# Turning the attention's value product, with two heads per step, in a two-block hybrid layer on one Trainium2 core

## The reference, cut to what matters

```python
# 8 heads "a" (window 128, with sinks) and 8 heads "b" with three branches;
# heads of 64, and 4 heads share a key/value group (2 groups of each)
o_a = banded_gqa(qa, ka, v_a, 128, rel_bias[:, :8], sinks)
p_c = softmax(q_b . k_cmp); o_cmp = p_c . v_cmp        # 31 compressed keys
o_sel = softmax(q_b . k_sel + bias) . v_sel            # causal, all 512 keys
o_win = softmax(q_b . k_win + bias) . v_win            # causal, window 512
gb = sigmoid(g_b + b_nsa_gate)                         # a gate per head and branch
o_b = gb0 * o_cmp + gb1 * o_sel + gb2 * o_win
y = concat([o_a * silu(z_a), o_b * silu(z_b)])
out = x + gate * (y @ w_out)
```

## Time and profile before

| | us |
|---|---|
| three executions | 1449.93, 1450.42, 1449.90 |
| median | 1449.93 |
| the profiled execution | 1452.35 |
| its span (first to last instruction) | 1450.6 |
| of it, the attention up to the first tile of `w_out` (195.4 to 315.5) | 120.1 |

### The profile page before, as it was taken

How to read it: one execution, slowest core, us unless ns; L and a number is a source line. 1 busy time by engine, 2 the same in 40 slices (tenths; PEclk the granted TensorE clock), 3 DMA queues, 4 the chain that set the end, 5 groups by cost and what they waited for, 6 DMA issues and landing times.

```text
span 1450.6 us, 18082 instructions
## 1 busy us (share of the span) xinstructions
PE 1424.3 (98%) x6880; PEld 1187.8 (82%) x6880; DVE 742.1 (51%) x1200; ACT 603.1 (42%) x1014; POOL 113.1 (8%) x133
## 2 busy tenths in 40 slices
PE   6999999999999999999999999999999999999998
PEld 5787879998888888888888888888888888888887
DVE  6733678855666434556445344443457433333342
ACT  5624677745333332333333344432355333333221
POOL 5303232100000000000000111100000000000000
PEclk9999999999999999999999999999999999999999
DMA  9996200113433333212213233343332333333321
GB/s 283 318 228 216 65 1 2 59 59 104 159 101 93 109 89 101 87 59 76 77 52 87 71 89 88 101 150 98 87 102 83 106 102 101 88 98 96 105 80 58
DMA packets 227824, 149.69 MB, mean 103 GB/s; under 512 B 5330, under 2 KB 216014, under 8 KB 227108
## 3 DMA queue, kind: packets, MB, share of 16 engines
q1 hardware_dynamic: 223588, 131.63, 31.4%
q0 software_dynamic: 4160, 17.04, 4.1%
HBM read 140.92 MB, written 6.68 MB: 102 GB/s over the span
## 4 chain that ended last, share of the span: by engine, by line
PE 93%; DMA 2%; DVE 1%; SPq 1%; ACT 1%; issue 1%; DVEq 0%; ACTq 0%
PE ps L436 70%; PE ps L2266 6%; PE ps L2292 3%; PE ps L2191 3%; PE ps L1857 3%; DMA w_raw<-in_w_in_dram 2%; PE ps L2278 2%; PE ps L1965 1%; PE ps L1926 1%; PE ps L2177 1%; PE ps L2176 1%; SPq L550 1%; PE ps L1998 0%; SPq L580 0%; PE ps L2146 0%
## 5 line engine op out<-in xcount | busy, mean ns | idle before, releaser
L456 DVE TENSOR_TENSOR w_lo<-w_raw,w_hi 128x1024 fp32r<-128x1024 f32 (+1 forms) x214 | 258.3, 1210 | 255.8 <-ACT w_hi L451 253.1
L451 ACT ACTIVATE w_hi<-w_raw 128x1024 fp32r<-128x1024 f32 (+1 forms) x214 | 219.5, 1034 | 14.7 <-PE ps L436 11.2
L502 ACT ACTIVATE temps<-ps 128x512 f32<-128x512 f32 x67 | 40.0, 597 | 238.8 <-PE ps L436 238.8
L436 PE MATMUL ps<-g_hi,w_hi 128*128 128x512 f32 x384 | 95.8, 392 | 0.0
L436 PE MATMUL ps<-g_hi,w_lo 128*128 128x512 f32 x384 | 94.9, 389 | 0.0
L436 PE MATMUL ps<-g_lo,w_hi 128*128 128x512 f32 x384 | 94.8, 389 | 0.0
L436 PEld LDWEIGHTS ps<-g_hi,w_lo 128*128 128x128 f32 x384 | 72.1, 188 | 15.0
L436 PEld LDWEIGHTS ps<-g_lo,w_hi 128*128 128x128 f32 x384 | 72.1, 188 | 15.0
L436 PEld LDWEIGHTS ps<-g_hi,w_hi 128*128 128x128 f32 x384 | 71.5, 188 | 14.6
L436 PE MATMUL ps<-f_hi,w_lo 128*128 128x512 f32 x288 | 71.1, 389 | 0.0
L436 PE MATMUL ps<-f_hi,w_hi 128*128 128x512 f32 x288 | 71.1, 389 | 0.0
(11 more groups left out here) (448 smaller groups left out, 2738.7 us busy)
## 6 DMA issues: line engine op xcount, KB each, us to landing
w_raw<-in_w_in_dram SPq DMA_DIRECT2D x107, 512.0 KB, 3.9
w_raw<-in_w_ff_gate_dram SPq DMA_DIRECT2D x22, 512.0 KB, 3.7
w_raw<-in_w_ff_up_dram SPq DMA_DIRECT2D x22, 512.0 KB, 3.8
w_ada_shift_scale<-in_w_ada_dram SPq DMA_DIRECT2D x16, 512.0 KB, 8.3
w_raw<-in_w_r_out_dram SPq DMA_DIRECT2D x16, 512.0 KB, 4.5
w_raw<-in_w_ff_down_dram SPq DMA_DIRECT2D x16, 512.0 KB, 3.9
w_ada_gate<-in_w_ada_dram SPq DMA_DIRECT2D x4, 1024.0 KB, 11.6
x_spill<-x_t POOLq DMA_DIRECT2D x2, 2048.0 KB, 10.1
```

The lines of the kernel that those rows point to most:

```text
L436: mm = pe.matmul(bank, w[:, slot, k], mov[:, at_k], start=first and n == 0 and k == 0, stop=last and n == 2 and k == kts - 1)
L451: act.activation(whi[:, slot, 0:kts], raw[:, slot, 0:kts], ACT.Copy).then_inc(hi_done, 1)
L456: nc.vector.tensor_tensor(wlo[:, slot, 0:kts], raw[:, slot, 0:kts], whi[:, slot, 0:kts].bitcast(F32), ALU.subtract).then_inc(lo_done, 1)
L502: act.activation(dst, ps[:, o % 4], func, scale=scale).then_inc(evac, 1)
```

## The change

Heads go two at a time through all engines ("pairs"; 48 of them, and a pair has the same keys and the same value group). The value product is turned: 64 columns of the values are the stationary operand, and the transposed probabilities (128 queries) are the moving one; one head of a pair writes PSUM partitions 0 to 63 and the other 64 to 127, so that the result has the queries on the free axis, as `w_out` needs it. It comes three pairs behind the scores where keys are 128 or 256 wide, two pairs behind where they are wider. The transposes of the finished blocks fall away. The coefficients (one per query and head) must now lie on the free axis: GpSimd widens them to 64 columns (`widen`), TensorE transposes them (4 per group), ScalarE copies them out, and VectorE multiplies with them (`combined`). The gating by silu moves to GpSimd (`y_gate`), save for the last half, which VectorE and GpSimd share. For widths up to 256 the two heads' transposed probabilities share a bank and are copied by one instruction. The compressed probabilities are scaled by GpSimd before their transposes, which move to pair 5; the compressed products come at pairs 8, 9, 11 and 12, two later than elsewhere in this form, and the gates' reciprocal at pairs 2 and 3. SyncE holds the fourth tile of `w_out` until the last value product.

```diff
+CTR_AT = 5
+CO_PE_AT = (8, 9, 11, 12)
+K_WINDOW_AT = (1, 2, 3, 4)
+Y_AT = (16, 19, 22, 31, 34, 43, 46, 49)
+PAIRS = N_ATT // 2
+COEF_AT = (9,) + tuple(range(10, PAIRS, 4))
...
+def pv_step(p):
+    return p + 2 if wide_pair(p) else p + 3
...
             for k in range(KT):
+                if k == 3:
+                    sp.wait_ge(m["pv_mm"], PAIRS)
                 load(None, 0, U_WO + k, w_out_v[:, :, k * P:(k + 1) * P])
...  GpSimd
-            for b in (1, 2):
-                for part in range(4):
-                    k_rest(b, part)
+            for part in range(4):
+                k_rest(1, part)
+            pool.wait_ge(m["csoft_done"], 4)
...
+            g.tensor_tensor(csc_heads, csc_heads,
+                            cden[:].rearrange("p g q -> p (g q)").unsqueeze(2).to_broadcast([P, 32, NC_PAD]),
+                            ALU.mult).then_inc(m["cpool_done"], 1)
+            pool.wait_ge(m["cpool_done"], 2)
+            for part in range(4):
+                k_rest(2, part)
...
+            def widen(G):
+                pool.wait_ge(m["cf_done"], G + 1)
...
+                g.tensor_copy(wide_of(G).rearrange("p t (h d) -> p t h d", h=2),
+                              coef[:, G % 2].rearrange("p (t h) -> p t h", h=2).unsqueeze(3).to_broadcast([P, 4, 2, HD])
+                              ).then_inc(m["cpool_done"], 1)
...
+            for i in range(NI - 1):
+                if i:
+                    y_gate(i, 0)
+                    widen(3 * i + 1)
+                    y_rest(i, 0)
+                add_branch(i, 1)
+                widen(3 * i + 2)
+                if i == 0:
+                    y_gate(i, 0)
+                add_branch(i, 2)
+                if i == 0:
+                    y_rest(i, 0)
+                y_gate(i, 1)
+                widen(3 * i + 3)
+                y_rest(i, 1)
...  TensorE
-                        mm = pe.matmul(ps[:, 4 + u.group % 2, u.head * HD:(u.head + 1) * HD], pt[:, t % 2, blk(b)],
-                                       proj[:, v, c:c + HD], start=b == 0, stop=b == blocks - 1)
+                    for half in range(2):
+                        mm = pe.matmul(ps[half * HD:half * HD + HD, 4 + u.group % 2, blk(n % 4)], proj[:, v, c:c + HD],
+                                       pt_of(n, half)[:, blk(b)] if wide_pair(n) else pt_of(n)[:, blk(half * blocks + b)],
+                                       start=b == 0, stop=b == blocks - 1)
...
+            for n in range(PAIRS + 1):
+                if n < PAIRS:
+                    scored(2 * n)
+                    scored(2 * n + 1)
+                if n == 0:
+                    v_local()
+                for p in (n - 3, n - 2):
+                    if p >= 0 and pv_step(p) == n:
+                        weighted(p)
+                if n >= 1:
+                    transposed(2 * n - 2)
+                    transposed(2 * n - 1)
+                if n == CTR_AT:
+                    compressed_transposed()
+                if n in CO_PE_AT:
+                    compressed_out(CO_PE_AT.index(n))
+                if n in COEF_AT:
+                    coefficients_wide(COEF_AT.index(n))
+            early_out(0)
+            weighted(PAIRS - 1)
+            coefficients_wide(N_GROUPS - 1)
```

More of the change, by code:

```diff
@@ L132, in __init__, with wide_pair, copies, buffers @@
         self.first_block = self.i + 1 - blocks
+def wide_pair(p):
+    return Step(2 * p).width > 2 * P
+def copies(p, engine):
+    return sum(wide_pair(n) or n % 2 == engine for n in range(p + 1))
+def pv_step(p):
+    return p + 2 if wide_pair(p) else p + 3
+def buffers():
+    of, last, c = [], {}, 0
+    for p in range(PAIRS):
+        n = 2 if wide_pair(p) else 1
+        c += c % n
+        used = tuple((c + k) % 4 for k in range(n))
+        of.append((used, max(last.get(b, -1) for b in used)))
+        last.update({b: p for b in used})
+        c += n
+    return of
+PT_BUFFERS = buffers()
 def norm_group(t):
@@ L1017, in _, with exponential @@
             act_out(act, None, 0, U_LAST, proj[:, VA], O_Z + 8, ACT.Copy)
-            for s in range(STEPS):
-                if s == 1:
+            def exponential(s):
+                G, n = divmod(s, 8)
+                u = att(s)
+                act.wait_ge(m["s_bias"], s + 1)
+                if n == 0 and G >= 2:
+                    act.wait_ge(m["cf_done"], G - 1)
+                a.activation(sc_of(s)[:, 0:u.width], sc_of(s)[:, 0:u.width], ACT.Exp, scale=-1.0,
+                             bias=row_min[:, G % 2, n:n + 1],
+                             accum_out=den[:, G % 2, n:n + 1]).then_inc(m["s_exp"], 1)
@@ new lines, in _ @@
+                if n == CONVERT_AT:
+                    act_convert(act, None, 0, U_LAST + AHEAD)
+                if n == CTR_AT + 1:
+                    act.wait_ge(m["aux_tr"], 1)
+                    a.activation(cpt[:, 0], ps[:, 6], ACT.Copy).then_inc(m["aux_ev"], 1)
+                for part, k in enumerate(K_WINDOW_AT):
+                    if n == k:
+                        k_round(2, part)
+                G, part = divmod(n, 4)
+                if part == 0 and G >= 1 and G <= N_GROUPS and (G - 1) % 3 == 0:
@@ new lines, in coefficients @@
+            def coefficients(G):
+                i, branch = divmod(G, 3)
+                cf, dn = coef[:, G % 2], den[:, G % 2]
+                dve.wait_ge(m["s_exp"], 8 * G + 8)
+                if branch == 0:
+                    dve.wait_ge(m["sinkexp_done"], i + 1)
+                    own(v.tensor_tensor(dn, dn, sink_exp[:], ALU.add))
+                    own.wait()
+                if G >= 2:
+                    dve.wait_ge(m["aux_tr"], G + 1)
+                if branch == 0:
+                    v.reciprocal(cf, dn).then_inc(m["cf_done"], 1)
+                    return
+                own(v.reciprocal(cf, dn))
+                own.wait()
+                v.tensor_tensor(cf, cf, gate_of(branch)[:, i], ALU.mult).then_inc(m["cf_done"], 1)
@@ new lines, in transposed @@
+            def transposed(t):
+                p, half = divmod(t, 2)
+                w = att(t).width
+                pe.wait_ge(m["s_exp"], t + 1)
+                before = p - 1 if wide_pair(p) or wide_pair(max(p - 1, 0)) else p - 2
+                if half == 0 and before >= 0:
+                    for engine, name in enumerate(("pt_d", "pt_a")):
+                        if copies(before, engine):
+                            pe.wait_ge(m[name], copies(before, engine))
+                for b in range(w // P):
+                    bank, c = (2 + half, b) if wide_pair(p) else (2 + p % 2, half * w // P + b)
+                    mm = trans(ps[:, bank, blk(c)], sc_of(t)[:, blk(b)])
+                mm.then_inc(m["t_mm"], 1)
```

448 lines of the change are left out of this document (223 added, 225 removed).

## The result

| | before | changed |
|---|---|---|
| median of four executions, us | 1449.91 | 1459.09 |
| lowest and highest | 1449.83, 1450.42 | 1457.62, 1459.99 |
| the profiled execution, its span | 1452.35, 1450.6 | 1458.33, 1456.6 |

The ratio is 1.0061 (95% interval 1.0046 to 1.0076): slower by 9.2 us, outside the predicted range of 1441 to 1455, and on the other side of the forecast. The changed kernel measured once more (e11) gave 1.0048 (1.0031 to 1.0065), 7.0 us slower, so 7 to 9 us are to be explained.

What follows compares the result with a forecast made beforehand. TensorE, busy for 98% of the span, was taken as the bound. Stretch terms +2.6, -1.5, -1.0, -3.6 and 0 sum to -3.5, turning the profiled 1452.35 into 1448.85; median forecast 1446.4, range 1441 to 1455.

Steps and rivals of the forecast that it cites:

- By stretch: Attention summed over stretches by key width, with pair prices and booked waits per group: -3.5 us in all.
- The five groups 256 wide: Attention stretch with keys 256 wide: 39.0 us against 40.5 before, 7.4 per group plus sinks and the last compressed product.
- widened coefficients wait on GpSimd: Rival: TensorE's coefficient turn stops for late `widen`, 0.6 per group, +7 us, 1453.5; chance 0.14.
- fits: GpSimd's new gates and widenings have room: 10.2 of 20 us were busy in the first stretch, far less behind.
- The clock: Rival: granted clock falls once more as TensorE is left open at step 16, costing 1.7 us, 1448.1; chance 0.11.
- The turned product: Attention's value product: 0.216 instead of 0.444 us per key block of two heads, 24.6 us less on TensorE.
- Loads exposed: Rival: 64-column weight loads can't run under a product, +11.9 us, 1458.3; chance 0.07.
- The change-over: Going into and out of the turned form on TensorE: 0.33 us per burst, 46 bursts, 15.2 us more.
- The pair prices: TensorE time per attention pair: 1.21, 1.60, 2.25 and 2.88 us at widths 128, 256, 384 and 512.
- Queries 0: First attention stretch, width 128: GpSimd's scaling delays the keys' rests and step 16; 22.6 us against 20.0, +2.6.
- The tail: First tile of `w_out`: five dependent operations outlast the other two parts by about 1 us; net 0.
- The rest: Behind the attention: second block untouched, SyncE's later `w_out` loads hidden by tiles; without that cover some 6 us.

Runs made afterwards that it cites:

- e11: The changed kernel unedited, measured once more beside e10: 1457.77 us, ratio 1.0048 to the kernel before.
- e7: e1 with the four compressed products at pairs 8, 10, 12, 14 instead of 8, 9, 11, 12: 1449.88 us, 2.4 less than e1.
- e6: e1 with VectorE's two weight conversions at pairs 42 and 44 (512 wide) instead of 31 and 32 (384 wide): 1451.28 us, 1.0 less than e1.
- e3a: The changed kernel plus one unused turned product per pair from pair 14, right behind the turned value product, as a control without added change-overs: 1461.43 us.
- e3: e3a and e3b together: the changed kernel with an unused turned product per pair, without and with its own change-over; 1461.43 and 1470.6 us.
- e5: e1 with the value products of an even and an odd pair in one burst at widths 128 and 256: 1449.22 us, 3.1 less than e1.
- e1: The changed kernel with TensorE's coefficient turn, ScalarE's copy and VectorE's combination one pair later in groups 1 to 9: 1452.32 us, ratio 1.0019.
- e3b: The changed kernel plus the same unused product as e3a, but between the two heads' transposes, where it needs its own change-over: 1470.6 us.
- e10: The changed kernel with only TensorE's coefficient turn moved, behind the next pair's scores; ScalarE's copy and VectorE's combination stay: 1456.37 us, ratio 1.0045.
- e8: e1 with the edits of e5, e6 and e7 together: 1446.86 us, ratio 0.9970 to the kernel before.

## Why the prediction was wrong

**The step that failed** is in "By stretch": "I book 0.6 of waits per group (0.35 at 512)". That was the allowance for a relay VectorE, GpSimd, TensorE, ScalarE, VectorE of which each leg had been costed, but whose start was never set against TensorE's place for the turn. The starts were there to be laid out: the coefficients follow a copy and precede the biases of the same pair, `widen` takes 0.61 behind them, and the turn closes that same pair. With pairs of 1.6 us that leaves the relay late. The five groups 256 wide took 44.2 (42.8 in e11, with the clock's fall elsewhere) where 39.0 were booked. The rival "widened coefficients wait on GpSimd" (1453.5, chance 0.14) had the right mechanism, but found against it that the additions end a pair earlier. That is true and beside the point: in four of the five groups in which `widen` was late nothing stood ahead of it. At 384 and 512 wide it was in time. Moving the relay by one pair gave 6.8 us by the medians (5.5 against e11); in the profiles it is 6.2 (126.9 against 120.7 from the first scores to the second tile), of which 1.4 is the fall of the clock at 234.5 (by e11) and 0.8 the shorter conversion (1.51 for 2.32).

**Two further waits were not in the sum.** Compressed products at neighbouring pairs in one PSUM bank (e7: 2.4 by the medians, 3.3 in the profiles), and two weight conversions at neighbouring pairs of a stretch where VectorE has no room (the group 12.38 against 10.11; e6 got back 1.0). The prediction looked at VectorE's load per pair and left out its work that comes once. And it found that GpSimd's new work "fits" by GpSimd's own room; that a gate could meet VectorE's conversion, and one of the two then takes 1.1 longer, was not in it.

**The clock** was a rival with one fall for 1.7 us (1448.1). In the medians it took 4.6 us by the estimate above, more than that rival allowed. The row that goes with it: in the first stretch TensorE was busy for 7.33 of the 10 us from 204.4, against 8.69 of the 10 from 205 in the earlier trace rows; yet in that profile the clock did not fall there, and in e11's it did.

**Right, term by term.**
- The turned product: four instructions take 0.22 (e3a) where 0.216 was booked, and 0.444 was the other bound. "Loads exposed" is refuted: from 300.40 to 301.43 sixteen take 1.03 with 0.16 of change-over in it.
- The Trainium skill ("TensorE: Matmul & The Clock Gate", Part 3, The mechanism) lets loads overlap products in flight only when the row group differs. The two halves share their rows, and sixteen instructions of 128 columns in 0.87 us are 0.054 each, half of L1998's 0.108 for half its columns. So the trace disagrees again with that rule. The same section also lets a load go ahead into the background weight buffer, and with that the trace agrees.
- The change-over: 0.29 to 0.34 by e3 and e5, 0.33 booked.
- The pair prices: 2.98 measured for 2.88 (the scores of two heads take about 0.95, not 0.82: 299.30 to 300.40 less half a change-over). In e1, groups 5 and 7 take 7.23 and 9.53 where 7.4 and about 9.9 were booked.
- Queries 0: 23.2 for 22.6. Step 16's scores came at 207.96, 13.6 after the first ones, as before; 14.0 was predicted, by the right chain (the scaling took 1.91, not 2.6). The excess lay in the products behind them.
- The tail: the predicted stall of about 1 before the last part is the 0.89 that L2280 waits for `y_lo`.
- The rest: from the second tile of `w_out` to the end it is 1135.4 us after and 1135.3 before. SyncE's new wait and the second block cost nothing.

**What stays open.** e1, with groups 4 to 7 as booked, still stood at 1452.3, not at 1446.4: the two waits above and the clock account for it roughly (1452.3 less 2.4 and 1.0 is 1448.9), not closely. How the 9.2 us divide between clock and waits in executions without a profile rests on a clock rounded to 0.001. Why e1 gained 1.1 us in groups 7 and 10, where `widen` was in time, isn't shown; ScalarE's copy and VectorE's combination moved there too. No kernel with pairs but an unturned value product was run, so the worth of the two parts of the change isn't separated. What sets the start of the attention between 193.0 and 195.4 was not looked into.

## What to carry to other kernels

A value that travels over four engines within a loop should be laid out as a relay, with start and end of each leg in the loop's own times, and its last taker placed behind the end with a pair's room to spare. In a kernel in which TensorE was open for 2%, work taken off it (here 7.7 us) is soon outweighed by waits of a few tenths in each group; they show in the chain of waits, not in the busy sums. Work that comes once or twice in a tight loop belongs at pairs that are not neighbours (e7, clear of the noise), and where the engine has room (e6, not clear of it). And work moved to an idle engine isn't free by that: look at what the other engines do at that moment.

## What the runs showed of the hardware

- Going from full-width operands to 64-column halves and back costs 0.29 us in this chain, half on each side, and it costs that although the operands were ready (e3b). Putting two pairs in one burst gets it back (e5, groups 5 and 6).
- A two-operand instruction of VectorE and one of GpSimd that met did not run side by side: a conversion of 1.22 took 2.32 when GpSimd's gate had started 0.03 before it, and the gate of 1.27 took 2.32 when the conversion had started 0.03 before it (e10). A sum over 8 columns took 0.88 and ended 0.02 behind GpSimd's instruction (changed kernel, 231.34); in the kernel before one took 1.09 and ended 0.03 behind one at 251.62.
- The granted clock differs between executions of the same kernel: in ten of e1 it was 0.997 at 1450.85 to 1452.33 us, 0.995 at 1452.38, 0.994 at 1454.92, 0.993 at 1456.55 and 0.991 at 1458.70. All kernels with the change had more of the low ones than the kernel before, but waits do not order them: 0.996 or more stood in 6 of 10 executions of e1 and in 3 of 8 of e8, the fastest. What brings a fall is not shown, and a profile shows only one execution.
